# Latent attention with values by tokens and packed weights, together with norms on columns of tokens and high parts first

## The reference

```python
cq, ckv, kr = split(h @ w_a, [384, 384 + 256])       # 672 columns
cq, ckv = rms_norm(cq, g_q), rms_norm(ckv, g_kv)
q = (cq @ w_uq).reshape(B, L, 16, 64 + 32)           # 64 plain, 32 rotary
kv = (ckv @ w_ukv).reshape(B, L, 16, 64 + 64)        # 64 of the key, 64 of the value
q_rope, k_rope = rotate(q[..., 64:]), rotate(kr)     # k_rope is shared by all heads
o = softmax(causal(qf @ kf.T / sqrt(96))) @ v
return o.reshape(B, L, 1024) @ w_o
```

## Time and profile before

| | us |
|---|---|
| median of three runs (lowest, highest) | 1401.75 (1399.26, 1403.01) |
| the profiled execution, its own time | 1404.32 |
| span of the profiled execution | 1402.4 |
| busy PE, PEld, DVE, ACT, POOL | 1336.0, 1267.9, 945.4, 811.3, 231.8 |
| granted TensorE clock, mean over the span | 0.982 of full |

### The profile page before, as it was taken

How to read it: one execution, slowest core, us unless ns; L and a number is a source line. 1 busy time by engine, 2 the same in 40 slices (tenths; PEclk the granted TensorE clock), 3 DMA queues, 4 the chain that set the end, 5 groups by cost and what they waited for, 6 DMA issues and landing times.

```text
span 1402.4 us, 30127 instructions
## 1 busy us (share of the span) xinstructions
PE 1336.0 (95%) x10433; PEld 1267.9 (90%) x10433; DVE 945.4 (67%) x1890; ACT 811.3 (58%) x1637; POOL 231.8 (17%) x216
## 2 busy tenths in 40 slices
PE   7899999999999999999986999999988999999997
PEld 6788999999977999999975899999987888999997
DVE  4665777765797777765685777776564566777754
ACT  5455676654666666654643567665463555766644
POOL 1000034420000044320010003442000000243400
PEclk9999999999999999999988999999998999999999
DMA  7332455556421456566330135655643333366662
GB/s 256 115 107 74 136 172 187 178 179 195 139 76 49 134 180 188 172 189 188 123 100 31 61 121 170 190 178 180 195 124 119 101 97 122 119 186 190 181 214 86
DMA packets 56867, 203.33 MB, mean 145 GB/s; under 512 B 6224, under 2 KB 8272, under 8 KB 56656
## 3 DMA queue, kind: packets, MB, share of 16 engines
q1 hardware_dynamic: 56784, 202.21, 46.1%
HBM read 201.13 MB, written 1.05 MB: 144 GB/s over the span
## 4 chain that ended last, share of the span: by engine, by line
PE 84%; DVE 7%; ACT 6%; issue 2%; DMA 1%; SPq 0%; DVEq 0%; ACTq 0%
PE ps L376 23%; PE ps L380 22%; PE ps L379 22%; PE ps L494 3%; PE ps L395 2%; PE ps L512 2%; PE ps L398 2%; PE ps L399 2%; DVE w_lo L1135 2%; PE ps L477 1%; PE ps L459 1%; ACT w_hi L765 1%; ACT probs L815 1%; DMA cst<-in_consts 1%; PE ps L577 1%
## 5 line engine op out<-in xcount | busy, mean ns | idle before, releaser
L1135 DVE TENSOR_TENSOR w_lo<-raw,w_hi 128x1024 fp32r<-128x1024 f32 x378 | 462.3, 1224 | 254.3 <-ACT w_hi L765 252.6
L376 PE MATMUL ps<-h_hi,w_hi 128*128 128x272 f32 (+1 forms) x1752 | 511.7, 292 | 7.7 <-DVE q_rope L1325 4.9
L765 ACT ACTIVATE w_hi<-raw 128x1024 fp32r<-128x1024 f32 x378 | 396.8, 1051 | 191.7 <-PE ps L376 180.0
L380 PE MATMUL ps<-h_hi,w_lo 128*128 128x272 f32 (+1 forms) x1752 | 504.8, 288 | 0.0
L379 PE MATMUL ps<-h_lo,w_hi 128*128 128x272 f32 (+1 forms) x1752 | 503.6, 287 | 0.0
L376 PEld LDWEIGHTS ps<-h_hi,w_hi 128*128 128x128 f32 x1752 | 330.8, 189 | 15.7 <-issue 5.9
L379 PEld LDWEIGHTS ps<-h_lo,w_hi 128*128 128x128 f32 x1752 | 331.4, 189 | 0.3
L380 PEld LDWEIGHTS ps<-h_hi,w_lo 128*128 128x128 f32 x1752 | 330.9, 189 | 0.0
L376 PE MATMUL ps<-hid_hi,w_hi 128*128 128x272 f32 (+2 forms) x676 | 198.1, 293 | 0.3 <-DVE y L1135 0.2
L379 PE MATMUL ps<-hid_lo,w_hi 128*128 128x272 f32 (+2 forms) x676 | 195.4, 289 | 0.0
L380 PE MATMUL ps<-hid_hi,w_lo 128*128 128x272 f32 (+2 forms) x676 | 195.4, 289 | 0.0
(11 more groups left out here) (153 smaller groups left out, 1751.2 us busy)
## 6 DMA issues: line engine op xcount, KB each, us to landing
raw<-in_weights SPq DMA_DIRECT2D x378, 512.0 KB, 3.7
cst<-in_consts SPq DMA_DIRECT2D x1, 1795.5 KB, 12.3
h<-in_x SPq DMA_DIRECT2D x2, 544.0 KB, 5.5
out<-h SPq DMA_DIRECT2D x8, 128.0 KB, 1.8
```

Of the source, the lines that this page charges most:

```text
L376: m = pe.matmul(b, whi, xhi, start=n == 0, stop=False)
L380: m = pe.matmul(b, wlo, xhi, start=False, stop=n == len(tiles) - 1)
L765: act.activation(w_hi[slot][:], raw[slot][:], ACT.Copy).then_inc(hi_ready, 1)
L1135: return dve.tensor_tensor(out_, a_, b_, op)
```

## The change

Two edits are made at once.

**Norms.** The sums over features are made with tokens in the partitions: the stationary operand is a block of 128 tokens of `totals` (or of the last tile, or of its square), the moving one a single column of `ones`, in three blocks (`THIRDS`), so that mean and mean square are 128 x 3 numbers. A matmul with a block of zeros opens each of the two banks. DVE forms the variance on 128 x 3, ACT takes Sqrt (its table is asked for where Ln's was), DVE the reciprocal, and PE spreads it back over the partitions with three matmuls against `ident` into PSUM bank 6, from where DVE's rescaling reads it. The mean for the centering is still made over 272 columns, but behind the columns. POOL centers six tiles and DVE two (`CENTER_DVE = 2`). The low part of the last unit moves from DVE to POOL, in front of its centering. The warming matmuls go from 28 to 12. `leading_from_h` does, for each tile, first the products with `h_hi` on `norm_hi`, and those with `h_lo` when `h_ready` comes.

**Latent layer.** Values are made with tokens in the partitions (`value_panel`): the latent is stationary, 512 columns of weights move, six panels of six matmuls, ahead of the loop; ACT copies them out with the reciprocal root as a scale by partition (`copy_vt`). `turn_value`, `copy_value` and DVE's share of the values go. The reciprocal root of the queries' latent goes into the mask's scale (`q_scale`), and ACT copies the queries' panels plainly (`take_q`). The roots are therefore also made as columns (`sum_squares` with nine and six column matmuls). All four rope panels stand ahead of the loop, the swaps of the last two at m = 1 and 3, their rotations at the end of m = 2 and 4. Rope and pair tiles are packed densely: nine units in place of ten. `mix(m-3)` stands at the head of an iteration, in place of `mix(m-2)` at its end.

```diff
-CENTER_DVE = 5
+CENTER_DVE = 2
-    "mla": [whole("a", 6), latent_pairs("qkv"), whole("o", 8, 4)],
+    "mla": [whole("a", 6), rope_head("r"), Stage("vt", [], 2, body=1), latent_pairs("qk"), whole("o", 8, 4)],
-WARM = 28
+WARM = 12
...
+            def leading_from_h(n, s, u0, p0, count, t0):
...
+                for k in range(DC - 1):
+                    pe.wait_ge(norm_hi, 8 * n + k + 1)
+                    for j, (b, slot) in enumerate(zip(banks, slots)):
...
+                        m = pe.matmul(b, w_hi[slot][:, at_k], h_hi[:, k, t0:T], start=k == 0, stop=False)
+                        pe.matmul(b, w_lo[slot][:, at_k], h_hi[:, k, t0:T], start=False, stop=False)
+                    pe.wait_ge(h_ready, 8 * n + k + 1)
+                    for b, slot in zip(banks, slots):
+                        pe.matmul(b, w_hi[slot][:, at_k], h_lo[:, k, t0:T], start=False, stop=False)
...
+                for b in (7, 4):
+                    pe.matmul(ps[:, b, 0:3], zero[:], zero[:, 0:3], start=True, stop=False)
+                def columns(b, src, last=False):
+                    for ch, (lo, hi) in enumerate(THIRDS):
+                        ins = pe.matmul(ps[:, b, ch:ch + 1], src[:, lo:hi], ones[:, 0:1],
+                                        start=False, stop=last and ch == 2)
                 pe.wait_ge(sums_added, 6 * (n + 1))
+                columns(7, totals[:, 0, :])
+                columns(4, totals[:, 1, :])
                 pe.matmul(ps[:, 5, 0:T], ones, totals[:, 0, :], start=True, stop=False)
-                pe.matmul(ps[:, 6, 0:T], ones, totals[:, 1, :], start=True, stop=False)
                 pe.wait_ge(bank_free, p0 + 8)
+                columns(7, h[:, 7, :], last=True).then_inc(mean_col_done, 1)
+                pe.wait_ge(squared, 8 * n + 8)
+                columns(4, squares[:, 1, :], last=True).then_inc(sq_mean_done, 1)
                 pe.matmul(ps[:, 5, 0:T], ones, h[:, 7, :], start=False, stop=True).then_inc(mean_done, 1)
-                pe.matmul(ps[:, 6, 0:T], ones, squares[:, 1, :], start=False, stop=True).then_inc(sq_mean_done, 1)
+                pe.wait_ge(rstd_done, n + 1)
+                for ch, c0 in enumerate((0, 0, P - TAIL)):
+                    ins = pe.matmul(ps[:, 6, lo:hi], col[:, 2, ch:ch + 1].broadcast_to([P, P]),
+                                    ident[:, c0:c0 + hi - lo], start=True, stop=True)
...
-                act.activation(mean_sq, ps[:, 5, 0:T], ACT.Square).then_inc(mean_squared, 1)
-                own.link(act.activation(rstd[:], rstd[:], ACT.Ln, bias=eps[:, 0:1]))
-                act.activation(rstd[:], rstd[:], ACT.Exp, scale=-0.5).then_inc(std_done, 1)
+                act.activation(col[:, 1, :], col[:, 1, :], ACT.Sqrt, bias=eps[:, 0:1]).then_inc(root_done, 1)
...
+            def norm(n, stage):     # POOL
+                    pool.tensor_tensor(w_lo[slot][:], raw[slot][:], w_hi[slot][:].bitcast(F32),
+                                       ALU.subtract).then_inc(lo_ready, 1)
...
+                    for n in range(6):                  # PE, latent layer
+                        value_panel(n)
+                        if n in (1, 3):
+                            swap_rope(n // 2)
+                    for r in range(2):
+                        panel(sq, uq, pq, 0, r, from_latent(0), None, 0)
                     for m in range(PAIRS + 1):
+                        if m >= 3:
+                            mix(a, kind, m - 3)
                         if m == 1:
+                            pe.wait_ge(vt_copied, 6)
+                            swap_rope(2)
                         if m == 3:
+                            swap_rope(3)
...
-            turn_value(m - 1, 7)
```

More of the change, by code:

```diff
@@ L97, in whole, with rope_head @@
     return Stage(name, [[(j, k, k) for k in range(DC)] for j in range(n)], n, body, banks, shift)
-PAIR_TILES = (Q_LORA // P, KV_LORA // P, KV_LORA // P)
-ROPE_AFTER = 2
-RK = Q_LORA // P
+QT, KT = Q_LORA // P, KV_LORA // P
+ROPE_PANELS = 4
+def rope_head(name):
+    return Stage(name, [[(0, r * QT + k, k) for k in range(QT)] for r in range(2)], 1, banks=2)
 def latent_pairs(name):
[L108 to L119, removed]
+    sizes = [QT] * (ROPE_PANELS - 2) + [QT, KT] * PAIRS
+    first = [sum(sizes[:j]) for j in range(len(sizes))]
+    panels = [[((f + k) // DC, (f + k) % DC, k) for k in range(n)] for f, n in zip(first, sizes)]
+    return Stage(name, panels, -(-sum(sizes) // DC), banks=2)
 DOWN_TILES = (8, 7, 7)
@@ L229, in c @@
             return cst[0:rows, a:b]
-        mean_sq, mean = y[:, 2, :], y[:, 3, :]
+        mean, rstd = y[:, 3, :], ps[:, 6, 0:T]
         ident, ones = c("ident"), c("ones")
@@ L409, in turn @@
                         if isinstance(i, int) and i == 0 and j < lead:
-                            if j == 0:
+                            if j == 0 and name in ("o", "down"):
                                 leading_panels(s, u0, p0, rhs, ready, lead, t0, range(led, DC))
+                            elif j == 0:
+                                leading_from_h(2 * layer + (name == "up"), s, u0, p0, lead, t0)
                         else:
@@ new lines, in take_q @@
+                    def take_q(m):
+                        p = pq + 2 + 2 * m
+                        act.wait_ge(panel_done, p + 1)
+                        for s in range(2):
+                            ins = act.activation(queries[0:HD, 2 * m + s, :], bank(p, 2)[HD * s:HD * s + HD], ACT.Copy)
+                        ins.then_inc(q_taken, 1)
+                    for r in range(2):
+                        take_r(r)
+                    split_unit(ur + AHEAD)
+                    for n in range(6):
+                        copy_vt(n)
+                        if n == 0:
+                            split_unit(uv + AHEAD)
@@ L1005, in _ @@
+                    split_unit(uv + 1 + AHEAD)
+                    for r in range(2):
+                        split_panel(a, "qk", r)
+                        take_r(2 + r)
                     for m in range(PAIRS + 1):
```

329 lines of the change are left out of this document (191 added, 138 removed).

## The result

The changed kernel takes 1446.45 us (median of four runs, 1435.28 to 1447.47) against 1402.17 (1399.26 to 1403.01): a ratio of 1.029, with a 95% interval of 1.0254 to 1.0327. It is slower by 44.3 us. The forecast was 1396.7, and the range ended at 1409.

A forecast was written before the change was run, and what follows sets the result against it. PE, busy 95% of the span, was taken to bound the kernel outside its interruptions in norms and latent layer. Norms +3.75 and latent layer -8.8 (+6.9 - 15.7) sum to -5.05 us: 1396.7 from the median 1401.75, range 1384 to 1409.

The forecast's parts named there:

- What costs nothing: the low part of the last unit on POOL.: Norms: POOL's 2.8 us operation ends near E + 1.5, far from its use after E + 7, so it adds nothing.
- POOL slowed by DVE: Rival, chance 0.05: POOL's centerings in the norms run at half pace beside DVE, 1.5 us each; together +6.3, 1403 us.
- PEclk 1.00 throughout: Sign expected in the profile after: PE's granted clock stays whole, at 1.00.
- the norm's columns let the clock fall: Rival, chance 0.14: single columns lower the clock, leading panels pay 1.7 us a norm, +12 in seven inner norms, 1408.7.
- The norm's other steps: Norms: column pass 0.11 us, variance at E + 4.1, rescaling E + 5.75, next stage E + 7.0; last norm +1.55.
- The latent prelude: Latent layer before the iterations: first scores come some 24.1 us behind stage a, with 1.5 of stage a inside: +6.9.
- The latent iterations: Latent layer, scores of m = 1 to m = 8: a chain through ACT bounds, 59.0 us against 74.7, so -15.7.
- the new gaps cost the clock: Rival, chance 0.16: PE's new latent-layer gaps halve the clock in the following pair, some 1.6 us each: +4.8, 1401.5.

The follow-up runs named there:

- The two runs that change only what PE does behind the sums: Kernel before with its 28 warming matmuls behind each inner norm's sums replaced by 14 single-column matmuls, or by nothing: 1415.74 us each, ratios 1.01 and 1.0103.
- The runs that removed the gaps: Latent part alone with later swaps and rotation behind the masks: 1402.89 us; then also ACT's splits behind its copies and high parts first: 1389.41 us, ratio 0.9905.
- The streams: Latent part alone with later swaps, plus three plain 272-column matmuls in front of each of six mixes: 1411.86 us, ratio 1.0070.

## Why the prediction was wrong

The 44.3 us in three pieces, each a difference of two kernels' medians: the latent part 9.6; the norm without POOL's low part 10.0 (1421.6 less 1411.56); POOL's low part on top of the columns 24.9. Forecast were -8.8 and, for all of the norm, +3.75.

**"What costs nothing: the low part of the last unit on POOL."** This step failed most. The cover was looked for at the end of the operation (its use after E + 7) and not beside it. Beside it stands DVE's last addition of the totals, which the sums wait for and which reads both its operands in SBUF. It takes 2.68 to 2.84 in place of 0.72, longer by 2.0 at each inner norm, 14 in all; alone in the old norm this costs 12.0. The Trainium skill ("Trainium Architecture — The Big Picture", What this means for kernel authors) calls the pair of ports that DVE and GpSimd share an exclusive lock and not a bandwidth split. The trace agrees: DVE's addition, begun 0.12 to 0.28 behind POOL's operation, ends 0.58 behind it at all seven norms, hardly less than the 0.72 that it takes alone. The prediction weighed the same sharing only the other way round, POOL slowed by DVE, as a rival of 0.05. Where POOL's centerings meet DVE's low parts, one centering did go from 0.76 to 0.97 (six take 4.35 in the last norm, 5.00 in the first), far from half pace, and such a low part from 0.49 to 0.60.

**"PEclk 1.00 throughout"** was wrong, and the rival *the norm's columns let the clock fall*, given 0.14, is what happened, with its mechanism: single columns behind dense weight loads didn't keep the clock up. The two runs that change only what PE does behind the sums show it. Even the rival's price was near, 1.7 a norm against 1.75. What it lacked was the compounding. Where a wait for POOL's operation stands ahead of the columns, the clock falls at seven norms of seven, at five of them in the columns (E + 2.8 to E + 3.9) and at two at their end or just behind them (E + 5.2 and E + 5.6). Then what is left of the columns, the sum for the mean, the spreading and the warming matmuls run at half pace, and these are the chain. Against the kernel with the low part on DVE the columns start 9.7 later in the seven norms together, and the next stages 19.9 later (78.1 against 58.2), so 10.2 is the low clock's. Another 5.3 between the two traces lies in the latent layer, where no instruction differs: the clock is at 0.50 for 36.9 us of its iterations against 23.7. That this part is POOL's doing isn't shown.

**The norm's other steps held.** A column pass is 0.12 (twelve in 1.48 or 1.40), forecast 0.11. In the last norm, where no low part runs, the variance starts at E + 3.86 (forecast E + 4.1), the rescaling at E + 5.61 (E + 5.75), and the last rescaling begins behind POOL's last centering:

```profile
1436.48 0.16 DVE L1256 TENSOR_TENSOR col<-ps,col 128x3 f32<-128x3 f32 x1 [0.38 <-PE ps L563]
...
1437.46 4.35 POOL L1207 TENSOR_TENSOR h<-h,y 128x272 f32<-128x272 f32 x6 [61.48 <-ACT y L932]
1438.23 2.67 DVE L1397 SCALAR_TENSOR_TENSOR h<-h,cst,ps 128x272 f32<-128x272 f32 x6
...
1441.84 0.50 DVE L1397 SCALAR_TENSOR_TENSOR h<-h,cst,ps 128x272 f32<-128x272 f32 x1 [0.22 <-POOL h L1207]
```

E to the end of the span is 13.06, before 11.73: +1.3, forecast +1.55. Where the clock holds, the next stage starts at E + 6.91; forecast E + 7.0.

**The latent prelude was mis-sized by 3.7.** Stage a grew by 3.1, forecast 1.5; the way from there to the first scores by 7.4, forecast 5.4 (the forecast's 24.1 has the 1.5 of stage a inside). The sum over columns in stage a, in the kernel with the latent part alone, and the stretch behind it (the row of before was one plain matmul of two passes, 0.73, behind a wait of 0.64 for the same square):

```profile
695.97 2.14 PE L677 MATMUL ps<-cst,y 128*128 128x1 f32 x18 [1.66 <-ACT y L996]
...
698.30:701.70 3.40, 3.40 (x18) 3.40 (x17) 2.56 (x3) 2.10 (x4) 0.00 (x0) 0.52 0.74 225
```

The columns themselves cost what was forecast. Behind them the clock is at 0.50 for 3.4 us, which is 1.7 of the 3.1: what the rival says of the norms, in stage a, again behind a wait (1.66). On the way to the first scores it stays whole in this kernel, so the 2.0 missing there are of the steps' sizes; which of them isn't worked out.

**The latent iterations were mis-sized by 12.9:** 71.9 in that kernel, forecast 59.0. Five of the seven came out within 1.8: 5.2, 13.3, 11.7, 7.8, 11.5, 12.8, 9.5 against 5.0, 12.3, 8.2, 7.2, 10.4, 8.2, 7.7, with PE waiting 2.48 in front of the swap at m = 3 and 4.04 for the mix behind m = 5, forecast 3 and 4. The two that are 3.5 and 4.6 too long lie behind these waits and run at 1.2 GHz (scores 3.78 for 2.15, turns 2.79 for 1.87). That is the rival *the new gaps cost the clock*, given 0.16; its +4.8 was too small, since it charged each gap one following pair of which the chain feels 1.6, and here the pair, the turns and the panel all lie in the chain. In all the clock is at 0.50 for 30.7 us of these iterations, so it can have cost up to 15.3, more than the whole miss. The runs that removed the gaps brought the iterations to 56.3 and the time at 0.50 in them to 6.8 us (high parts first has no part in it: alone it leaves the old iterations at 74.6). Of the 15.5 gained at most 12.0 is clock, so at least 3.5 is the gaps themselves. The streams left the clock as it was and so tell nothing of the two apart.

So in the latent layer too the step that failed first is "PEclk 1.00 throughout", behind two waits whose places and lengths were forecast nearly right (2.48 and 4.04 for 3 and 4).

What stays open: why the clock held at two norms of seven in the kernel with the low part on DVE, where all seven have the same instructions; what the latent layer's scatter owes to chance, since the same iterations took 75.6, 71.9, 70.2 and 68.9 us in the four kernels that have them unchanged, in one trace each; and why the streams at the mixes didn't lift it.

## What to carry to other kernels

When an operation moves to POOL, look at what DVE does in the same stretch: a two-operand addition on SBUF waited here until POOL's operation was over, so the moved work is only free where DVE has nothing on the path. Replacing wide matmuls by single-column ones may keep PE's records dense, but here the granted clock fell as if PE had stood still; count the half-clock time behind it, above all if a wait stands ahead of it. And a stall whose cause is one instruction's place in an order (here the rotation at DVE's end of an iteration) is to be tried by moving that instruction before the layer is laid out anew: two moved calls and high parts first gave 1.44%, the new layout with all its orders mended and the same high parts 0.95%.

## What was not expected of the hardware

POOL's subtraction of 128x1024 takes 2.38 us and holds back a DVE addition of 128x544, which then takes 2.67 to 2.85 us in place of 0.72 (seven of seven in each kernel that has it). Twenty-eight float32 passes with one moving column, PE busy for 3.18 to 3.86 us in the records, leave the clock where no instruction at all leaves it: 1415.74 us with either, PEclk at the fourth norm 0.76 and 0.75, then 0.50.
